# Last layer's second feed-forward product as a seven-product block scheme (Strassen), token-major

## The reference, cut to what matters

```python
x = x + jnp.einsum('bse,ed->bsd', mixed, w_o[l])
h = rmsnorm(x, mlp_norm[l])
u = jnp.square(jax.nn.relu(jnp.einsum('bsd,df->bsf', h, w_ff1[l])))   # 512 x 4096
x = x + jnp.einsum('bsf,fd->bsd', u, w_ff2[l])                        # 4096 -> 1024
...
return rmsnorm(x, final_norm)
```

## Time and profile before

| | us |
|---|---|
| median of 3 runs | 2709.9 (2709.84 to 2710.2) |
| span of the profiled execution, first to last instruction | 2708.0 |
| TensorE busy (matmuls) | 2687.0, 99% |
| VectorE busy | 1551.6, 57% |
| ScalarE busy | 1154.0, 43% |
| GpSimd busy | 681.2, 25% |
| DMA | 87 GB/s over the span |

### The profile page before, as it was taken

How to read it: one execution, slowest core, us unless ns; L and a number is a source line. 1 busy time by engine, 2 the same in 40 slices (tenths; PEclk the granted TensorE clock), 3 DMA queues, 4 the chain that set the end, 5 groups by cost and what they waited for, 6 DMA issues and landing times.

```text
span 2708.0 us, 32235 instructions
## 1 busy us (share of the span) xinstructions
PE 2687.0 (99%) x12902; PEld 2250.4 (83%) x12902; DVE 1551.6 (57%) x2312; ACT 1154.0 (43%) x1836; POOL 681.2 (25%) x695
## 2 busy tenths in 40 slices
PE   8999999999999999999999999999999999999999
PEld 7888888888888888888888888788888888788887
DVE  6656554344466646665575668644445558655444
ACT  4323423222347636532235767522224667522223
POOL 1000111011136626400004753411103553511100
PEclk9999999999999999999999999999999999999999
DMA  4332232323222222223322221233333211233332
GB/s 160 97 101 93 91 108 93 101 95 100 90 75 61 67 75 67 86 95 101 100 94 88 82 67 40 79 101 97 98 94 103 78 57 54 71 101 94 97 98 78
DMA packets 69414, 238.80 MB, mean 88 GB/s; under 512 B 7696, under 2 KB 10256, under 8 KB 69264
## 3 DMA queue, kind: packets, MB, share of 16 engines
q1 hardware_dynamic: 69264, 236.73, 28.1%
HBM read 234.60 MB, written 2.10 MB: 87 GB/s over the span
## 4 chain that ended last, share of the span: by engine, by line
PE 91%; DVE 4%; POOL 2%; ACT 2%; issue 0%; DMA 0%; SPq 0%; ACTq 0%; DVEq 0%
PE ps L416 29%; PE ps L418 29%; PE ps L417 29%; POOL wl L2419 2%; PE ps L552 1%; PE ps L777 1%; PE ps L776 1%; PE ps L485 0%; DVE wl L1636 0%; ACT wh L1018 0%; PE ps L613 0%; PE ps L612 0%; DVE xl L1648 0%; PE ps L470 0%; PE ps L452 0%
## 5 line engine op out<-in xcount | busy, mean ns | idle before, releaser
L1018 ACT ACTIVATE wh<-raw 128x1024 fp32r<-128x1024 f32 (+2 forms) x453 | 465.2, 1028 | 730.7 <-PE ps L418 723.7
L416 PE MATMUL ps<-xh,wh 128*128 128x512 f32 x1920 | 751.7, 391 | 0.2 <-POOL wl L2419 0.2
L418 PE MATMUL ps<-xh,wl 128*128 128x512 f32 x1920 | 747.4, 389 | 0.0
L417 PE MATMUL ps<-xl,wh 128*128 128x512 f32 x1920 | 747.2, 389 | 0.0
L1636 DVE TENSOR_TENSOR wl<-raw,wh 128x1024 fp32r<-128x1024 f32 (+1 forms) x339 | 447.7, 1321 | 156.9 <-ACT wh L1018 156.5
L416 PE MATMUL ps<-yh,wh 128*128 128x512 f32 x1088 | 425.3, 391 | 1.9 <-POOL wl L2419 1.9
L416 PEld LDWEIGHTS ps<-xh,wh 128*128 128x128 f32 x1920 | 360.5, 188 | 76.2 <-issue 1.0
L417 PE MATMUL ps<-yl,wh 128*128 128x512 f32 x1088 | 423.5, 389 | 0.0
L418 PE MATMUL ps<-yh,wl 128*128 128x512 f32 x1088 | 423.4, 389 | 0.0
L418 PEld LDWEIGHTS ps<-xh,wl 128*128 128x128 f32 x1920 | 360.4, 188 | 75.1
L417 PEld LDWEIGHTS ps<-xl,wh 128*128 128x128 f32 x1920 | 360.6, 188 | 74.8 <-issue 1.0
(11 more groups left out here) (267 smaller groups left out, 3628.6 us busy)
## 6 DMA issues: line engine op xcount, KB each, us to landing
raw<-in_ff SPq DMA_DIRECT2D x120, 512.0 KB, 3.6
raw<-in_pool_in SPq DMA_DIRECT2D x64, 512.0 KB, 3.3
raw<-in_conv_in SPq DMA_DIRECT2D x64, 512.0 KB, 3.3
raw<-in_pool_out SPq DMA_DIRECT2D x32, 512.0 KB, 3.3
raw<-in_qk SPq DMA_DIRECT2D x32, 512.0 KB, 3.7
raw<-in_pool_grp SPq DMA_DIRECT2D x16, 512.0 KB, 3.3
raw<-in_conv_out SPq DMA_DIRECT2D x16, 512.0 KB, 3.3
raw<-in_mla_z SPq DMA_DIRECT2D x16, 512.0 KB, 3.6
```

Source lines behind the costliest of these rows:

```text
L416: pe.do.matmul(o, lh, rh_, start=start, stop=False)
L417: pe.do.matmul(o, lh, rl_, start=False, stop=False)
L418: return pe.do.matmul(o, ll, rh_, start=False, stop=stop)
L1018: act.do.activation(h[:, 0:ncol], r[:, 0:ncol], ACT.Copy).then_inc(*mark("whi", ("whi", k)))
```

## The change: what it does

For the last layer, each quarter's f2 is split in a two by two scheme over hidden channels (halves of 512, blocks 0 to 3 and 4 to 7), tokens (halves of 256) and output columns (halves of 512). Seven products per quarter take the place of eight. The left operands are two pieces of y directly or with one of four sums t1 to t4; the right operands are four weight pieces A11, A12, A21, A22 or four sums S1 to S4 of them. Every product is a sum over four blocks of 128 hidden channels for two token blocks of 128 with 512 output columns: 4 x 2 x 3 = 24 matmuls, and uses two weight units (kk = 0, 1) of 128 x 1024. Three chains of results stay in PSUM: A (Q1, Q6, Q7, Q4, each accumulated onto the one before), C (W5, Q3) and B (Q2). After each product VectorE adds or subtracts the bank to a token-major block `zblock`, kept in the memory of `x` (`post`); in an accumulated chain TensorE waits for that (`zp`) before it goes on in the same bank.

What else moves: the f1 order in layer 1 becomes 0, 4, 1, 5, 2, 6, 3, 7, so that the sums t of blocks k and k + 4 can be made during f1 (`t_sums`, `t_low` on VectorE, `t_high` on ScalarE). S1 and S3 are summed by VectorE during f1, S2 and S4 during the products (`wsum`). Squares go from GpSimd to ScalarE (`ff_square`). `x` is turned in quarter 0, four token blocks after f1 number 4 and four after number 5 (numbers count from 0), and copied out after numbers 5 and 6 in ScalarE's list (`turned_in`). SP loads the four pieces (eight DMAs of 512 KB per quarter) straight into memory that attention used (`G`, `SETS`). In quarter 3 the row ends are `row_square`, `row_scale`, `row_first`, `row_second`. The cut diff:

```diff
+FF_ORDER = (tuple(range(8)), (0, 4, 1, 5, 2, 6, 3, 7))
+PRODUCTS = ("Q1", "W5", "Q6", "Q2", "Q7", "Q3", "Q4")
+WEIGHT_OF = {"Q1": "A11", "W5": "S1", "Q6": "S2", "Q2": "A12", "Q7": "S3", "Q3": "S4", "Q4": "A22"}
+CHAIN_OF = {"Q1": "A", "W5": "C", "Q6": "A", "Q2": "B", "Q7": "A", "Q3": "C", "Q4": "A"}
+CHAIN_BEFORE = {"Q6": "Q1", "Q7": "Q6", "Q4": "Q7", "Q3": "W5"}
...
 TensorE
+                        if l == 1 and qd == 0 and n in (4, 5):
+                            turn_x(n - 4)
...
+            def turn_x(half):
+                for tb in range(4):
+                    b = bank("ox", tb, half)
+                    for i in range(4):
...
+            def quarter(qd):
+                for name in PRODUCTS:
+                    ns = [unit["zq", qd, name, kk] for kk in range(2)]
+                    chain, before = CHAIN_OF[name], CHAIN_BEFORE.get(name)
+                    if before is None:
+                        for tb in range(2):
+                            bank("z" + chain, qd, tb)
+                    steps = [(kk, kp, tb) for kk in range(2) for kp in range(2) for tb in range(2)]
+                    if qd == 3 and name == "Q4":
+                        steps = [(kk, kp, tb) for tb in range(2) for kk in range(2) for kp in range(2)]
+                    for kk, kp, tb in steps:
+                        wh, wl = unit_ready(ns[kk])
+                        k = 2 * kk + kp
+                        if k == 0 and before is not None:
+                            pe.wait_ge(*at("zp", qd, before, tb))
...
 ScalarE, in each quarter of layer 1
                 for qd in range(4):
+                    for n, i in enumerate(FF_ORDER[l]):
                         taking("f1", l, qd, i)
...
+                        weights(unit["f1", l, qd, i] + AHEAD[min(n, 4) if qd == 0 else 4])
...
+                        if n and n % 2 == 0:
+                            t_high(qd, n // 2 - 1)
+                        ff_square(qd, i)
+                        ff_high(qd, i)
+                        if qd == 0 and n in (5, 6):
+                            turned_in(n - 5)
...
+                        t_high(qd, 3)
+                        for name in PRODUCTS:
+                            for kk in range(2):
+                                taking("zq", qd, name, kk)
+                                if qd == 3:
+                                    last_rows(name, kk)
...
+            def last_rows(name, kk):
+                if name == "Q7":
+                    row_square(0, kk, 16)
+                elif name == "Q3":
+                    row_square(1, 2 + kk, 16)
+                elif name == "Q4":
+                    row_square(0, 2 + kk, 20)
+                    row_scale(0, 2 + kk)
...
 VectorE
+                def t_sums(qd, k):
+                    y, y4 = temp("ff", l, qd, k), temp("ff", l, qd, k + 4)
+                    t1, t2, t3, t4 = [TS[:, 256 * n:256 * n + 256] for n in range(4)]
...
+                def quarter(qd):
+                    for n, name in enumerate(PRODUCTS):
+                        for kk in range(2):
+                            taking("zq", qd, name, kk)
+                            if n:
+                                post(qd, PRODUCTS[n - 1], kk)
+                            if name == "Q1":
+                                wsum(qd, "S2", kk, "S1", "A11")
+                            if name == "Q6":
+                                wsum(qd, "S4", kk, "S2", "A12")
+                            if qd == 3 and name in ("Q3", "Q4"):
+                                row_first(0 if name == "Q3" else 1, kk if name == "Q3" else 2 + kk)
+                    if qd == 3:
+                        row_second(0, 2)
+                        row_second(0, 3)
+                    for tb in range(2):
+                        post(qd, "Q4", tb)
+                        if qd == 3:
+                            row_second(1, tb)
...
 VectorE, in each iteration of f1
+                        if qd == 0 and n:
+                            ff_low(0, FF_ORDER[l][n - 1])
+                        if l == 1 and n and n % 2 == 0:
+                            t_sums(qd, n // 2 - 1)
+                        weights(unit["f1", l, qd, i] + AHEAD[min(n, 4) if qd == 0 else 4])
+                        if l == 1 and n and n % 2 == 0:
+                            t_low(qd, n // 2 - 1)
+                        if l == 1 and n in (3, 5):
+                            wsum(qd, "S1", n // 4, "A21", "A22")
+                        if l == 1 and n in (4, 6):
+                            wsum(qd, "S3", n // 5, "A21", "A11")
+                        if qd or n == 7:
                             ff_low(qd, i)
```

More of the change, by code:

```diff
@@ L196, in unit_table @@
                     low(False)
[L197 to L200, removed]
[L201 to L202 removed]
+            if l == 0:
+                out_units("f20", D["ff20"], qd)
+            else:
+                for name in PRODUCTS:
+                    for kk in range(2):
+                        add(("zq", qd, name, kk), (qd, name, kk), 1024)
     for n, u in enumerate(units):
@@ L208, in unit_table @@
         u.append(on)
-    return units, index
+    loaded = [n for n, u in enumerate(units) if not isinstance(u[0], tuple)]
+    slots = {n: (i % NRAW, loaded[i - NRAW] if i >= NRAW else None) for i, n in enumerate(loaded)}
+    return units, index, slots
 def temp_table():
@@ L944, in turn_x @@
[L944 to L972, removed]
@@ new lines, in post @@
+                def post(qd, name, tb):
+                    half, tok, sign = POST[name]
+                    z = zblock(half, 2 * tok + tb)
+                    dve.wait_ge(*at("mm", "zq", qd, name, tb))
+                    if qd == 0:
+                        dve.wait_ge(*at("xt", half, 2 * tok + tb))
+                    if name in POST_BEFORE:
+                        dve.wait_ge(*at("zp", qd, POST_BEFORE[name], tb))
+                    p = ps("z" + CHAIN_OF[name], qd, tb)[:, :]
+                    done = [("zp", qd, name, tb)]
+                    if name in CHAIN_LAST:
+                        done.append(("psfree", "z" + CHAIN_OF[name], qd, tb))
+                    if qd == 3 and name in ("Q2", "Q7", "Q3", "Q4"):
+                        done.append(("z", half, 2 * tok + tb))
+                    if sign > 0:
+                        dve.do.tensor_tensor(z, p, z, ALU.add).then_inc(*mark("dve", *done))
+                    else:
+                        dve.do.tensor_tensor(z, z, p, ALU.subtract).then_inc(*mark("dve", *done))
@@ new lines, in second_layer, with row_first @@
+                        if qd or n == 7:
+                            ff_low(qd, i)
+                    if l == 0:
+                        out_proj("f20", qd, 6 if qd == 3 else None)
+                    else:
+                        t_sums(qd, 3)
+                        t_low(qd, 3)
+                        quarter(qd)
+            def row_first(half, tb):
+                dve.wait_ge(*at("zs", half, tb))
+                dve.do.tensor_scalar(sc(24, tb), sc(16, tb), 1.0 / 1024, EPS, ALU.mult, ALU.add).then_inc(
+                    *mark("dve", ("zsum", tb)))
+                z = zblock(half, tb)
+                dve.wait_ge(*at("fn"))
+                dve.do.tensor_tensor(z, z, FN[:, half * S:half * S + S], ALU.mult).then_inc(*mark("dve", ("zf", tb)))
```

267 lines of the change are left out of this document (177 added, 90 removed).

## The result

Before 2709.87 us (median of 4, 2709.69 to 2710.2), after **2723.43 us** (median of 4, 2722.42 to 2724.06): ratio 1.0049, 95% interval 1.0035 to 1.0064. The change makes the kernel slower by 0.5%; predicted were 2724.2. The profiled span went from 2708.0 to 2721.2 us, +13.2, where the prediction had +14.3.

A forecast was written before the change was run, and what follows sets the result against it. The prediction took TensorE, busy 2687.0 of 2708.0 us, to bound the kernel. Its terms, -21.8 + 14.5 + 2.6 + 12.6 + 6.4 = +14.3, gave a span of 2722.3 and 2724.2 us timed, range 2711 to 2735.

The forecast's parts named there:

- Removed: Last layer's second product: 96 of 768 matmuls go, at 0.2267 us each, 21.8 us less for TensorE.
- Place 1: Turning x in quarter 0: TensorE waits for VectorE's evacuations and a ninth bank of eight, 14.5 us more.
- The clock: After the waits at the turns of x, TensorE's clock falls: 13 matmuls at half speed, 2.6 us more.
- Place 2: Start of each product stage: TensorE waits for the (W5,1) residual and Q1's posts, 12.6 us over four quarters.
- Place 3: The tail: a wait in Q4, then four serial row ends after the last matmuls, 6.4 us more.
- The drain: VectorE residuals: the skill's drain would repeat them every 2.2 us; the prediction used the trace's 1.14 us instead.
- (a): Rival: TensorE keeps its feed, only unavoidable waits remain, -17.4 us, span 2692.5; chance 7%.
- (b): Rival: the bank wait at the turns holds, product stages run free, -1.7 us, 2708; chance 9%.
- (c): Rival: VectorE paces the products, 12 in-place hand-overs (Q6, Q7, Q4) lose 0.7 us more each, 2732; chance 17%.

The follow-up runs named there:

- The second experiment: Changed kernel with the residual of (W5,1) moved ahead of t_low of block 3 and the S2 sums; 2719.35 us, 1.0034 against the kernel before.
- the kernel of 2699.99 us: Changed kernel with x turned earlier, (W5,1) residual earlier, row ends reordered, quarter 0's S1 and S3 sums earlier, weights split less far ahead; 2699.99 us, 0.9962.

## Why the prediction was right

- **Removed, 21.8 us.** 96 matmuls went, and where nothing waits the pitch stayed 0.227 us: right.
- **Place 1, 14.5 us.** The same way of counting: f1 number 4 ends 0.27 before the rounding at 2378.04, number 6 would start 9.24 later at 2387.0 and starts at 2401.82: 14.8. The three stops came as said, behind the named instructions: 1.42 (1.3), 4.21 (4.4), 6.84 (7.6). The rest is mostly the twelve transposes between the last two stops: they take 3.19 us (sixteen took 1.91), as the granted clock is 0.50 there. They cost nothing by themselves, since the last stop would have been longer by as much. Evacuation 3 starts at 2390.28, the working had 2389.5 (done 2390.2): late by 0.8, of which 0.6 was there before the turns (below). The early turns confirm it by 9.8 us net, the split less far ahead separates its halves.
- **The clock, 2.6 us.** That it falls at place 1 was right, when and for how many matmuls was not. It falls at 2390.1, in the stop of 4.21 us, and is back at 2403.8, so that most of the slow time is spent on transposes and on waiting. After the 6.84 us wait six matmuls take 2.38 us (2401.82 to 2404.20) instead of 1.36, so 1.0, not thirteen's 2.6. A second one that the prediction lacks follows the 2.28 us wait of quarter 0: eight matmuls take 3.47 us (2424.36 to 2427.83) instead of 1.81, 1.7. Together 2.7: the total came out by chance.
- **Place 2, 12.6 us.** Quarter 0 costs 4.1 (4.2 predicted), but by 2.28 of wait, the restart and the slow matmuls, with no wait at Q6; the other three 2.8 each (2.8) by waits of 1.29 (1.6) and 0.70 (1.2); start to start shows 0.8 more than these two, since a matmul behind a wait runs 0.50 and not 0.39 and smaller stops are not listed. Sum 12.6, of which 1.7 is the slow matmuls just counted: the agreement with 12.6 is again partly chance, as the waits alone were put too high. The second experiment shows the order: take the W5 wait away, and Q6's grows.
- **Place 3, 6.4 us.** Q4 waits 0.94 and restarts, 1.2 (1.3). The last matmul is over at about 2710.5, 2709.3 without that wait, and the span ends 11.9 later, against 6.0: 5.9. The last final scalings stand 2.66 and 2.67 apart, as said.
- **Sum.** -21.8 + 14.8 + 2.7 + 10.9 (place 2 without its slow matmuls) + 5.9 = +12.5, and 0.6 more below: 13.1 of the 13.2 measured. All other products and f1 blocks run start to start at the full pitch, so nothing else is lost. The 0.6 is there before the change's first instruction in time (evacuation 0 starts at 2374.72, before at 2374.09). It lies inside what executions differ by, and is not put down to the change: in four more kernels with the same program up to there the reciprocal ahead of it starts at 2370.39, 2370.66, 2371.05 and 2371.83, against 2370.60 before and 2371.22 in the changed kernel.
- **The drain.** The prediction set the Trainium skill's drain (VectorE: DVE Perf Modes, The DRAIN you can't avoid) against the trace's 1.14 us. The same section says that an instruction that is not held starts earlier, so the two need not disagree; the sum did not use it.
- **Rivals.** (a) and (b) need place 1 or place 2 to be cheap, and neither was. (c) wanted a loss at each in-place hand-over: there is none at Q7 in any quarter and one at Q4, in the last, for a residual and not for a post. The 0.1 us of room that the working gave it there held; how large it is in truth was not measured. With the squares on GpSimd the time is near (c)'s 2732, by another way: at W5 and at the turns, not at Q7 and Q4.

What the prediction did not see is that its terms were not independent: TensorE's wait at the banks was also the time in which VectorE caught up. With both halves of it gone a wait of 4.10 us comes up in Q1, of which the early turns' later norm may be a part; with one half gone (6.3 us) none does. That does not show in the sum of this kernel, only when a term is taken away.

Open is whether an order exists that has neither the bank wait nor the backlog: none of the eleven kernels has it.

## What to carry to other kernels

A saving on the engine that bounds a kernel is worth what the feeding engines can follow: here a scheme with one eighth fewer matmuls needs twice the weight units per matmul time and sums beside them, and it is the order in the feeders' queues that loses the time, at a VectorE load of 61%. Count banks and buffers in flight at the moved step first (the ninth of eight still cost a wait of 7.3 us with the other half of place 1 gone, sixteen weight sums 4.2), and look at what stands ahead, in program order, of the instruction that gives one back. Before a wait is removed, ask which engine has been using it to catch up: its backlog is the next wait.

## What the runs showed of the hardware

The granted clock falls after far shorter stops than the 6.46 us of the start. TensorE of the changed kernel in six stretches (window and length; busy us of PE, PEld, DVE, ACT, POOL with counts; granted clock; DMA share; GB/s):

```profile
2378.00:2390.00 12.00, 7.40 (x40) 5.88 (x38) 5.86 (x9) 5.15 (x7) 0.00 (x0) 1.00 0.35 125
2391.00:2394.30 3.30, 3.08 (x12) 2.28 (x12) 3.30 (x7) 1.26 (x2) 0.00 (x0) 0.50 0.00 0
2394.30:2401.00 6.70, 0.00 (x0) 0.00 (x0) 5.19 (x8) 3.75 (x7) 0.00 (x0) 0.50 0.00 0
2401.00:2405.00 4.00, 3.95 (x14) 3.35 (x15) 0.00 (x0) 1.46 (x3) 0.00 (x0) 0.65 0.00 0
2424.00:2430.00 6.00, 5.64 (x18) 4.55 (x19) 4.91 (x6) 2.30 (x3) 0.00 (x0) 0.72 0.00 0
2430.00:2440.00 10.00, 10.00 (x46) 8.29 (x45) 9.34 (x10) 3.36 (x5) 0.00 (x0) 1.00 0.32 102
```

A single wait of 2.28 us, in a stage where TensorE had worked without rest for 20 us, is followed by seven matmuls at about 0.43 us pitch, which is 1.2 of 2.4 GHz; at 2427.8 the clock is 1.00 again. The Trainium skill (TensorE: Matmul & The Clock Gate, Part 1) has the fall after idle time and the return after sustained work; these two stretches agree. In the first product stage of the kernels run here the fall came with waits of 2.23, 2.27, 2.28, 2.38 (with 0.70 or 0.71 behind it), 2.63, 3.26 and 4.10 us, and with one of 1.47 with 0.71 behind it; it did not come with 1.74 or 1.75, nor with 1.35 or 1.33 with 0.71 behind. The stop of 2.28 us costs 1.7 us on top of itself; Q1 with the stop of 4.10 in it loses 2.7 more than its two waits.

The stop is not the whole cause, though. Here is a stretch long before the changed part, first in the kernel before, then in the profile of the kernel of 2699.99 us:

```profile
2246.00:2249.00 3.00, 3.00 (x15) 2.47 (x14) 2.96 (x12) 3.00 (x8) 0.00 (x0) 1.00 0.00 0
```

```profile
2246.00:2249.00 3.00, 3.00 (x16) 2.50 (x17) 2.97 (x12) 3.00 (x8) 0.00 (x0) 0.50 0.00 0
```

Nothing of the change comes before this stretch, TensorE was busy for 9.40 of the 10 us from 2234 on in both, and the only stop named ahead of it is one of 0.60 us in both. Yet the second has half the clock from 2244.5 for 6.8 us. That profile's execution took 2702.59 us, 2.6 more than the median of its kernel. A difference of 1 to 3 us between two profiles can be this, and is to be checked against the granted clock before it is explained.

VectorE's fp32 adds take longer in the groups that run beside GpSimd's work: a 1024-column sum takes 1.22 us alone and 1.74 on average in the group beside squares, a 256-column one 0.42 and 0.89; and VectorE's 512-column residual beside GpSimd's adds 1.13 instead of 0.69. How much GpSimd loses by it no run shows, as its adds were not timed alone.
